# Finishing the last two expert blocks apart, with all other rows loaded, normed and stored one block sooner

## What is computed

```python
hx = _rmsnorm(x, norm2[l]) * (1.0 + cx2) + sx2
x = x + gx2 * _moe(hx.reshape(-1, D), ...).reshape(x.shape)
return _rmsnorm(x, norm_f)
# _moe: the 2048 (row, expert) pairs are sorted by expert, each expert padded to blocks of 128 rows
def expert_block(args):
    xblk, e = args
    return (jax.nn.silu(xblk @ w1[e]) * (xblk @ w3[e])) @ w2[e]
y = (yb[dest] * wts.reshape(-1)[order][:, None]).astype(xf.dtype)
return jnp.zeros_like(xf).at[tok].add(y)
```

## Time and profile before

| | us |
|---|---|
| median of 3 runs | 955.77 (954.93 to 956.76) |
| the profiled execution, its own time | 955.9 |
| its span, first to last instruction | 954.1 |
| PE busy in it | 874.5 (92%) |
| DVE busy | 633.6 (66%) |
| ACT busy | 405.7 (43%) |
| POOL busy | 197.6 (21%) |
| DMA moved | 194.50 MB, mean 204 GB/s |

### The profile page before, as it was taken

How to read it: one execution, slowest core, us unless ns; L and a number is a source line. 1 busy time by engine, 2 the same in 40 slices (tenths; PEclk the granted TensorE clock), 3 DMA queues, 4 the chain that set the end, 5 groups by cost and what they waited for, 6 DMA issues and landing times.

```text
span 954.1 us, 15437 instructions
## 1 busy us (share of the span) xinstructions
PE 874.5 (92%) x5567; PEld 737.0 (77%) x5568; DVE 633.6 (66%) x876; ACT 405.7 (43%) x559; POOL 197.6 (21%) x211
## 2 busy tenths in 40 slices
PE   4999999999999899999469999999999999999870
PEld 1789876878897577887468988988898898898760
DVE  1568545689867647555784759499855745799933
ACT  3574454301224431221421556377542543676621
POOL 3232000000000110110011323243422313334233
PEclk8899999999999999999659999999999999999995
DMA  9846345601135033122947769889989669699775
GB/s 341 307 141 180 112 133 156 195 14 50 41 133 178 4 129 111 67 90 89 338 155 261 245 191 335 258 288 381 378 249 308 208 172 321 195 349 365 259 218 212
DMA packets 81156, 194.50 MB, mean 204 GB/s; under 512 B 3978, under 2 KB 12303, under 8 KB 81114
## 3 DMA queue, kind: packets, MB, share of 16 engines
q1 hardware_dynamic: 70624, 158.87, 47.7%
q0 software_dynamic: 7616, 25.06, 10.6%
q10 hardware_dynamic: 2874, 10.01, 2.7%
HBM read 168.50 MB, written 25.71 MB: 204 GB/s over the span
## 4 chain that ended last, share of the span: by engine, by line
PE 37%; DMA 6%; DVE 4%; issue 1%; ACT 1%; POOL 1%; SPq 0%; DVEq 0%; ACTq 0%; POOLq 0%
PE ps L2005 22%; PE ps L2016 7%; PE ps L2021 4%; DMA raw<-in_w_dram 3%; PE ps L1999 2%; DMA arena<-x_rows 1%; DMA x_rows<-arena,block_dst 1%; PE ps L1988 1%; DVE w3l L1540 0%; PE ps L2034 0%; DMA out_dram<-arena 0%; PE ps L2055 0%; ACT w3h L987 0%; SPq L576 0%; PE ps L1942 0%
## 5 line engine op out<-in xcount | busy, mean ns | idle before, releaser
L2005 PE MATMUL ps<-w3h,xTh 128*128 128x256 f32 x368 | 105.9, 288 | 0.0
L2005 PE MATMUL ps<-w3h,xTl 128*128 128x256 f32 x368 | 104.2, 283 | 0.0
L2005 PE MATMUL ps<-w3l,xTh 128*128 128x256 f32 x368 | 104.1, 283 | 0.0
L1540 DVE TENSOR_TENSOR w1l<-raw,w1h 128x2048 fp32r<-128x2048 f32 x30 | 68.6, 2287 | 29.4 <-ACT w1h L987 29.4
L987 ACT ACTIVATE w1h<-raw 128x2048 fp32r (+1 forms) x32 | 61.1, 1912 | 58.6 <-PE ps L2021 46.2
L2005 PE MATMUL ps<-w2h,hTh 128*128 128x512 f32 x184 | 76.9, 418 | 1.1 <-DVE hTl L1553 0.5
L2016 PE MATMUL ps<-w1h,xTh 128*128 128x512 f32 x184 | 73.7, 401 | 4.3 <-issue 3.0
L987 ACT ACTIVATE w2h<-raw 128x2048 fp32r (+1 forms) x32 | 61.1, 1917 | 31.0 <-PE ps L2005 22.3
L2016 PE MATMUL ps<-w1l,xTh 128*128 128x512 f32 x184 | 73.5, 400 | 0.0
L2005 PE MATMUL ps<-w2h,hTl 128*128 128x512 f32 x184 | 72.2, 392 | 0.0
L2005 PE MATMUL ps<-w2l,hTh 128*128 128x512 f32 x184 | 72.2, 392 | 0.0
(11 more groups left out here) (347 smaller groups left out, 2175.7 us busy)
## 6 DMA issues: line engine op xcount, KB each, us to landing
raw<-in_w_dram SPq DMA_DIRECT2D x48, 2048.0 KB, 13.3
arena<-in_w_mod_dram SPq DMA_DIRECT2D x32, 512.0 KB, 3.7
arena<-in_x_dram SPq DMA_DIRECT2D x16, 512.0 KB, 9.5
arena<-in_w_in_dram SPq DMA_DIRECT2D x8, 1024.0 KB, 6.4
arena<-in_w_mod_dram SPq DMA_DIRECT2D x3, 2048.0 KB, 13.5
x_rows<-arena ACTq DMA_DIRECT2D x9, 512.0 KB, 4.0
hx_rows<-arena ACTq DMA_DIRECT2D x9, 512.0 KB, 4.2
wo_f<-in_w_out_dram SPq DMA_DIRECT2D x2, 2048.0 KB, 8.5
```

What stands on the lines that cost most here:

```text
L1540: dve.tensor_tensor(half_of(j, w_lo[j][:, :], k), half_of(j, raw[:, bass.ds(base, UNIT)], k), half_of(j, w_hi[j][:, :], k).bitcast(F32), A ...
L2005: ins = pe.matmul(out_ap, parts[l][:, lhs], w_parts[w][:, cols], start=start and n == 0, stop=stop and n == 2)
```

## The change

`m = last - 1` takes the place of `last`: here 21. What it does:

- One place of `ysb` in place of two. POOL waits for the scatter of block `b-1` and frees the place ahead of `gather(b+2)`.
- POOL's loop ends with block `m-1` (20). The gather of block `m+1` (22) stands behind the loop, and so behind `add_rows(20)`. PE, ACT and DVE take block 21 in their loops as before.
- `rows_added` is set after the scatter of block 20. SP loads the eight tiles then, to places 0 and 1 of `raw`, and the gain `norm_f` behind them.
- ACT squares tiles 0 to 5 ahead of block 22's silu, tiles 6 and 7 behind it. DVE finishes tiles 0 to 4 ahead of the hidden rows of block 22, the others between them.
- `add_rows(21)` waits for the eight loads and stands behind the roots of tiles 0 to 5. When it has landed, POOL gathers the rows of block 21 (`rows_m`) and of block 22 (`rows_last`) from `x_rows`. `rows_m` is normed and scattered to `out`; then `rows_last`, plus the weighted rows of block 22, is normed and scattered over it.

The core of the diff:

```diff
@@ sync
-            for done in w_split:
-                sp.wait_ge(done, 2 * NE)
-            sp.dma_start(nfb, norm_f...).then_inc(S["nf_loaded"], 16)
-            sp.wait_ge(S["rows_added"], 1)
-            for t in range(NX):
-                sp.dma_start(x2[:, t, :], x_dram[t * P:(t + 1) * P, :]).then_inc(row_loaded[t], 16)
+            sp.wait_ge(S["rows_added"], 1)
+            sp.wait_ge(w_split[2], 2 * (NE - 1))
+            sp.wait_ge(w_split[0], 2 * NE)
+            for t in range(NX):
+                sp.dma_start(x2[t], x_dram[t * P:(t + 1) * P, :]).then_inc(row_loaded[t], 16)
+            sp.wait_ge(w_split[1], 2 * NE)
+            sp.dma_start(nfb, norm_f...).then_inc(S["nf_loaded"], 16)
@@ gpsimd
-                    with pool.If(i + (s + 1) < last):
+                    with pool.If(i + (s + 1) < m):
                         b = i + (s + 1)
-                        with pool.If(b + 1 < last):
+                        pool.wait_ge(S["y_added"], 16 * b)
+                        pool.sem_inc(S["y_free"], 1)
+                        with pool.If(b + 1 < m):
                             pool.wait_ge(S["x_turned"], b + 2)
                             gather(b + 2)
                         pool.wait_ge(S["y_ready"], 2 * i + (2 * s + 6))
                         pool.sem_inc(S["load_seen"], 1)
-                        pool.wait_ge(S["y_added"], 16 * b)
-                        pool.sem_inc(S["y_free"], 1)
-                        add_rows(b, 1 - s)
-            pool.wait_ge(S["y_added"], 16 * last)
+                        add_rows(b)
+            pool.wait_ge(S["x_turned"], m + 1)
+            gather(m + 1)
+            pool.wait_ge(S["y_added"], 16 * m)
             pool.sem_inc(S["rows_added"], 1)
...
+            pool.sem_inc(S["y_free"], 1)
+            root(0, 1)
+            root(1, 1)
+            root(2, 2)
+            root(4, 2)
+            pool.wait_ge(S["y_ready"], 2 * m + 4)
...
+            for t in range(NX):
+                pool.wait_ge(row_loaded[t], 48)
+            add_rows(m)
+            root(6, 2)
+            pool.wait_ge(S["y_added"], 16 * m + 16)
+            pool.sem_inc(S["y_free"], 1)
+            pool.wait_ge(w_split[1], 2 * NE)
...
+            root(NX, 1)
+            for par in range(2):
+                pool.wait_ge(stored[par], 16 * NX // 2)
+            pool.wait_ge(S["fout_ready"], NX + 1)
+            write_rows(rows_m, block_dst)
+            root(NX + 1, 1)
+            pool.wait_ge(S["y_added"], 16 * m + 32)
...
+            pool.wait_ge(S["fout_ready"], NX + 2)
+            write_rows(rows_last, block_tok)
+            pool.wait_ge(S["y_added"], 16 * m + 48)
@@ vector
+            for t in range(5):
+                finish(t, x2[t])
+            hidden(m + 1, 0)
+            finish(5, x2[5])
+            hidden_low(m + 1, 0)
+            hidden(m + 1, 1)
+            finish(6, x2[6])
+            hidden_low(m + 1, 1)
+            finish(7, x2[7])
+            finish(NX, rows_m)
+            weigh(m + 1)
...
+            dve.tensor_tensor(rows_last, rows_last, ysb, ALU.add).then_inc(S["last_sum"], 1)
+            finish(NX + 1, rows_last)
```

More of the change, by code:

```diff
@@ L223, in hybrid_block @@
         hsil = at(O_E + D + HALF, None, HALF)
-        ysb = at(O_E + 2 * D, "p (s n) -> p s n", 2 * D, s=2)
-        x2 = at(0, "p (t n) -> p t n", NX * D, t=NX)
-        nfb, sqf, last_x, last_out = (at(3 * UNIT + n * D, None, D) for n in range(4))
+        ysb, sqf = (at(O_E + (2 + n) * D, None, D) for n in range(2))
+        x2 = [at(t * D, None, D) for t in range(NX)]
+        nfb, rows_m, rows_last = (at(2 * UNIT + n * D, None, D) for n in range(3))
         ident = sb("ident", [P, P])
@@ L725, in _, with root @@
[L725 to L732, removed]
+            pool.sem_inc(S["y_free"], 1)
+            def root(t, n):
                 pool.wait_ge(S["fss_ready"], t + n)
@@ L1018, in _ @@
                 for s in range(2):
-                    with act.If(i + s < last):
+                    with act.If(i + s < m + 1):
                         b = i + s
@@ L1052, in _, with square_row @@
                             hidden_high(b, 1)
[L1054 to L1057, removed]
+            def square_row(t):
                 act.wait_ge(row_loaded[t], 48)
@@ L1060, in _ @@
                     act.wait_ge(S["fss_ready"], t)
-                act.activation(sqf, x2[:, t, :], ACT.Square, accum_out=stat[:, t:t + 1]).then_inc(S["fss_ready"], 1)
+                act.activation(sqf, x2[t], ACT.Square, accum_out=stat[:, t:t + 1]).then_inc(S["fss_ready"], 1)
+            for t in range(6):
+                square_row(t)
+            gate_up(m + 1)
+            square_row(6)
+            square_row(7)
+            hidden_high(m + 1, 0)
+            hidden_high(m + 1, 1)
+            act.wait_ge(S["gathered"], 16 * m + 48)
+            act.sem_inc(S["load_seen"], 1)
+            act.wait_ge(S["fss_ready"], NX)
+            act.activation(sqf, rows_m, ACT.Square, accum_out=stat[:, NX:NX + 1]).then_inc(S["fss_ready"], 1)
             act.wait_ge(S["last_sum"], 1)
-            act.wait_ge(S["fss_ready"], NX)
-            act.activation(sqf, last_x, ACT.Square, accum_out=stat[:, NX:NX + 1]).then_inc(S["fss_ready"], 1)
+            act.wait_ge(S["fss_ready"], NX + 1)
+            act.activation(sqf, rows_last, ACT.Square, accum_out=stat[:, NX + 1:NX + 2]).then_inc(S["fss_ready"], 1)
         @block.vector
@@ L1554, in hidden_low, with weigh @@
                     .then_inc(S["hT_b" if k else "hT_a"], 1)
-            def weigh(b, s, pair):
+            def weigh(b):
                 dve.wait_ge(S["l2_done"], b + 1)
@@ L1571, in _ @@
                 for s in range(2):
-                    with dve.If(i + s < last):
+                    with dve.If(i + s < m + 1):
                         b = i + s
@@ L1585, in _ @@
                             low(1, place[1] * UNIT, e + 1, 1)
-                            weigh(b, s, pair)
+                            weigh(b)
                             low(2, place[2] * UNIT, e + 1, 0)
@@ L1594, in _, with finish @@
                             turn_out(b + 1)
-                            weigh(b, s, pair)
-            def finish(t, src, dst):
+                            weigh(b)
+            def finish(t, row):
                 dve.wait_ge(S["fpow_ready"], t + 1)
-                dve.scalar_tensor_tensor(out=dst, in0=src, scalar=stat[:, 2 * NT + t:2 * NT + t + 1],
+                dve.scalar_tensor_tensor(out=row, in0=row, scalar=stat[:, 2 * NT + t:2 * NT + t + 1],
                                          in1=nfb, op0=ALU.mult, op1=ALU.mult).then_inc(S["fout_ready"], 1)
-            for k in range(2):
-                hidden(last, k)
-                hidden_low(last, k)
             dve.wait_ge(S["nf_loaded"], 16)
[L1606 to L1614, removed]
+            for t in range(5):
[9 more added lines that the diff above has]
+            weigh(m + 1)
+            dve.wait_ge(S["y_ready"], 2 * m + 6)
+            dve.wait_ge(S["last_loaded"], 16)
+            dve.tensor_tensor(rows_last, rows_last, ysb, ALU.add).then_inc(S["last_sum"], 1)
+            finish(NX + 1, rows_last)
         @block.tensor
```

57 lines of the change are left out of this document (31 added, 26 removed).

## The result

The changed kernel takes 962.75 us (median of 4 runs, 962.2 to 963.0), the kernel before 956.26 beside it: ratio 1.0066, 95% interval 1.0046 to 1.0086. It is slower, by 6.5 us. The profiled execution has a span of 960.5 against 954.1.

A forecast was written before the change was run, and what follows sets the result against it. The last 50 us, transfers and short operations in a line, were taken as the bound; +8.8 us on the span (7.4 late gather and clock, 1.4 longer line) over the 955.77 median gave 964.6 us, range 958.5 to 970.5.

The forecast's parts named there:

- The late gather: POOL after its loop: gather of block 22 starts at 894.4, so PE stops 5.7 us in block 21 (3.0 to 6.4).
- the rule that the prediction weighed there: POOL's copy for the late gather: DVE's instruction locks the shared port pair, so the copy ends with it at 893.6.
- The clock: PE after its stop in block 21: a lower granted clock costs 1.7 us, from nothing to 7.3.
- Squares and roots: ACT and POOL behind block 21: six squares of tiles 0 to 5 take 7.5 us, a two-tile root 2.2, until 924.1.
- The scatter of block 21: POOL, queued behind the roots of tiles 0 to 5: starts at 925.9, lands 9 us later at 934.9.
- The gather of its rows: POOL behind the scatter of block 21: landing 7.0 us (4.3 to 7.7), so landed at 942.8.
- The second rival: Late gather, scatter of block 21 and gather of its rows land fast; faster if these and the clock fall 10.7; 6%.
- Weighing, sum, square, root, finish behind the finish of block 21's rows: Block 22's rows at the end: 1.41, 1.23, 1.25, 0.95 and 1.25 us after 946.3, plus 0.1 steps, until 952.6.
- The loop: Block loop with one place of weighted rows: scatter landings and later gathers stay hidden, cost taken as 0.
- Without the gather still 1.4 slower: New line at the end: without the late gather and the clock it would still be 1.4 us longer than the old.
- The fourth rival: PE's clock stays low longer after the stop: up to 5.6 us more, 970; upper side of the forecast's range, no separate chance.

The follow-up runs named there:

- the first experiment: The changed kernel with only the gather of block 22 put back in POOL's loop, ahead of the scatter of block 20; 955.34 us, ratio 0.9989 to the kernel before.
- the third experiment: The kernel before with only one place of weighted rows, the scatter of block b-1 waited for ahead of the gather of b+2; 955.26 us, ratio 0.9985.
- the last three experiments: Block 22 weighed first, gather put back: 955.12 us; changed kernel with block 21's scatter ahead of the roots: 959.06; both orders, gather put back: 953.88.
- The last of them: On the gather-back, weighing-first kernel: scatter of block 21 ahead of all roots but two, hidden rows of block 22 ahead of DVE's finishes; 953.88 us, ratio 0.9969.

## Why the prediction was right

The forecast was 964.6, slower, by the late gather; measured 962.75. The two experiments that move this gather alone, one out of the changed kernel (7.4 us less) and one into the kernel before (6.5 us more), carry the cause. The nearness of the number is partly luck: block 21 ended 2.1 us later than forecast and the line behind it was 4.5 shorter, which leaves 2.4 on the span (960.5 against 962.9). Term by term, on the trace:

- **The late gather.** Start forecast at 894.4, found at 897.41; stop forecast at 5.7 us, found at 7.06, outside the 3.0 to 6.4 I had bounded. Of the 3.0 us by which the gather was later than forecast, 1.55 were there at the scatter of block 20 already (889.75 against 888.20), while PE wanted the rows only 0.8 later. The rest is POOL: the empty blocks took the 3.9 us given and 0.25 more to the copy, the copy took 2.29 where I had 1.5 (it ended at 896.24, with DVE's subtraction of 893.91 to 896.20, as by the rule that the prediction weighed there), and the step to the gather 1.2 where I had 0.8. My bounds for the stop had varied the landing alone and no term of POOL's. The landing, 6.15 us, was under my 7.0.
- **The clock.** Forecast 1.7. From the start of the turn to the end of block 21 it was 8.87 us against 7.51 before, so 1.4 more, and 1.8 more than the 7.08 of the first experiment (896.06 to 903.14). The end of block 21 that the forecast began from, 903.0, was 0.2 short: its last matmul starts at 902.83 and takes 0.39.
- **Squares and roots.** ACT's first square came 3.9 after PE's end (4.0); from it to the copy for the scatter 10.0 us (9.7 forecast); copy and step 1.0 (1.8).
- **The scatter of block 21.** 8.01 (9 forecast, bounds 5.9 to 13.0).
- **The gather of its rows.** This is the term that was mis-sized: 7.0 taken, 4.2 found, under every gather of the trace before. At 936 most stores have landed; the last is there by 937.9. The first experiment, in which the same gather starts at 925.06 among the stores and takes 7.93, shows that my 7.0 was not out of reach. The second rival had its mechanism right in its three transfers, each shorter than I took it, but by 0.8, 1.0 and 2.8 us together, 4.6 of the 10.7 it needed.
- **Weighing, sum, square, root, finish behind the finish of block 21's rows.** From 942.62 to the last scattered store at 950.76, 8.1 us; forecast the same way 8.5. So the line from block 21's end to the end of the span, forecast at 52.5 us, was 48.0 (960.5 - 912.5), while block 21 ended 2.1 later than forecast (912.5 against 910.4).
- **The loop** at nothing: the third experiment agrees.
- **"Without the gather still 1.4 slower".** This fell. With the gather put back the kernel was 1.4 us faster than before, 0.1%, so within what can't be told. In that experiment's trace the line from block 21's end (903.14) to the end of the span (953.1) is 50.0 us, 2.5 shorter than the 52.5 of the forecast: squares and roots up to the copy 8.4 instead of 9.7, copy and step 1.0 instead of 1.8, the scatter 7.72 instead of 9, and against that the gather 7.93 instead of 7.0. So it is mostly POOL's roots and copy, quicker than I took them, and not the landings, which nearly cancel.
- The fourth rival, a clock that stays low, did not come: at 908 to 910 it was full again.

Where did the 18 us by which the row loads are earlier (900.3 instead of 918.4) go? Stores and loads did leave the chain. But the rows of block 21, which the tiles no longer carry, put a scatter, a gather, a norm and a scattered store of their own in their place, and the last rows wait for that line twice: for DVE, and for the store that they overwrite. In the changed kernel the first decides (the last store waits for DVE's finish); the store of block 21's rows is on the chain in the last three experiments. The last of them took 2 us out of it by order alone. What stays open is how short the line could be if the gain of the norm were loaded ahead of the tiles, or block 21's rows were not written on their own; neither was tried.

## What to carry to other kernels

When a loop on an in-order engine is cut one round shorter, look at which side of the last round's work each of its prefetches lands: here the last gather went from ahead of a scatter to behind it, and this alone cost 0.64%, although the code read as the same sequence. Loads that start 18 us sooner are worth what the longest line behind them leaves, and a scatter that must land before its rows are read again makes such a line. And when an operation is moved ahead in a queue, what it passes is moved behind it and may hold the next step of the same line.

## What the runs showed of the hardware that I had not expected

The issue of a gather on POOL took 1.00 us before and 2.81 in the changed kernel, 2.95 in the first experiment. DVE was in a subtraction of two SBUF operands from 897.04 to 899.33, and the issue, begun at 897.41, ended at 900.22. Where the subtraction began only after the issue, as at 881.40 in the kernel before for the issue at 880.73, the issue kept its 1.00. The page "SBUF — State Buffer" of the Trainium skill (section on the two separate sides) says that GpSimd can't write descriptors while DVE runs in a 2-port mode, which holds the port pair that both share. Of a `tensor_tensor` with two SBUF inputs its section on who interferes with whom says that it contends with GpSimd's reads, and that it was not seen to stall a DMA. Here the issue did grow beside such a `tensor_tensor`, so for it the rows go further than the page; whether the reading of the row numbers or the writing of descriptors was held, no run tells. The landing counted from the start of the issue did not grow with it: the gather of block 21 took 7.0 us to land with an issue of 3.02 us in the first experiment, and 7.0 with one of 1.00 in the kernel before.

The landing of one and the same kind of transfer, 128 rows of 4 KB gathered by POOL, ranged in the changed kernel from 4.2 to 8.9 us; the trace before had shown 4.3 to 7.7. The gather of block 21's rows took 4.2 us in the changed kernel, where the core moved 249 GB/s from 936 to 940, and 7.93 in the first experiment, where it moved 359 GB/s from 925 to 933. No run varies the traffic beside it alone.
